# A hybrid encoder layer: one-hot picks per tile in the router's pipeline, and attention's levels ahead of the layer norm's tail

## What is computed

```
h = rms_norm(x);  q,k,v,r,gates,glu = split(h @ w_in)
a = gated linear attention, both directions, 4 heads, per-head norm, times silu(r)
b = silu(layer_norm(depthwise_conv31(glu_a * sigmoid(glu_g))))
x = x + concat(a, b) @ w_out
x = x + cross_attention(rms_norm(x), rms_norm(mem))      # 4 heads
h = rms_norm(x)
logits = h @ router_w + router_b                          # 1024 x 32
top_vals, top_idx = top_k(logits, 4);  gates = softmax(top_vals)
# tokens sorted by expert into blocks of rows; each block goes through its expert:
hid = min(g,7) * sigmoid(1.702 * min(g,7)) * (clip(l,-7,7) + 1)   # g,l = halves of x @ w_up[e] + b_up[e]
x = x + sum over the 4 picks of gate * (hid @ w_down[e] + b_down[e])
y = rms_norm(x)
```

## Time and profile before

| | us |
|---|---|
| median of 3 runs | 2631.83 (2628.87 to 2635.72) |
| profiled execution, own time | 2631.96 |
| its span in the trace | 2630.2 |
| TensorE busy | 2385.0 (91%) |
| VectorE busy | 1825.1 (69%) |
| ScalarE busy | 1286.7 (49%) |
| GpSimd busy | 363.0 (14%) |

### The profile page before, as it was taken

How to read it: one execution, slowest core, us unless ns; L and a number is a source line. 1 busy time by engine, 2 the same in 40 slices (tenths; PEclk the granted TensorE clock), 3 DMA queues, 4 the chain that set the end, 5 groups by cost and what they waited for, 6 DMA issues and landing times.

```text
span 2630.2 us, 38944 instructions
## 1 busy us (share of the span) xinstructions
PE 2385.0 (91%) x13604; PEld 1936.6 (74%) x13605; DVE 1825.1 (69%) x1912; ACT 1286.7 (49%) x1435; POOL 363.0 (14%) x305
## 2 busy tenths in 40 slices
PE   6999886699979967999999999999999999999993
PEld 4889664598748945777777777787787777777772
DVE  4699678514142276878977778778777788988763
ACT  5412255313231133656756565556565556766553
POOL 0000000010000032121212111121122112222111
PEclk7999998799999868999999999999999999999996
DMA  4211311310100138989988797789787789999775
GB/s 139 64 49 49 113 34 34 129 57 33 48 1 1 51 108 308 310 305 327 359 282 266 252 319 251 235 269 331 258 276 243 242 294 312 337 362 314 250 248 160
DMA packets 263969, 527.23 MB, mean 200 GB/s; under 512 B 10909, under 2 KB 45009, under 8 KB 263537
## 3 DMA queue, kind: packets, MB, share of 16 engines
q1 hardware_dynamic: 246976, 470.49, 50.9%
q0 software_dynamic: 15008, 52.70, 8.7%
q10 hardware_dynamic: 1904, 2.90, 0.4%
HBM read 484.37 MB, written 41.68 MB: 200 GB/s over the span
## 4 chain that ended last, share of the span: by engine, by line
PE 78%; DVE 10%; issue 5%; ACT 4%; DMA 1%; DVEq 1%; ACTq 0%; POOLq 0%; POOL 0%; SPq 0%
PE PS L2497 12%; PE PS L2499 11%; PE PS L2498 11%; PE PS L2064 9%; PE PS L2505 7%; PE PS L2502 6%; PE PS L2296 4%; PE PS L2394 4%; DVE wlo L1856 2%; PE PS L2467 1%; PE PS L2356 1%; PE PS L2321 1%; PE PS L2322 1%; PE PS L2323 1%; PE PS L2521 1%
## 5 line engine op out<-in xcount | busy, mean ns | idle before, releaser
L1856 DVE TENSOR_TENSOR wlo<-raw,whi 128x2048 fp32r<-128x2048 f32 x387 | 880.0, 2288 | 198.6 <-ACT whi L1116 175.7
L1116 ACT CAST whi<-raw 128x2048 fp32r<-128x2048 f32 x387 | 730.5, 1911 | 177.1 <-PE PS L2505 137.2
L2497 PE MATMUL PS<-whi,xhi 128*128 128x512 f32 x1024 | 426.2, 416 | 1.0 <-DVE wlo L1856 0.9
L2499 PE MATMUL PS<-whi,xlo 128*128 128x512 f32 x1024 | 401.6, 392 | 0.0
L2498 PE MATMUL PS<-wlo,xhi 128*128 128x512 f32 x1024 | 400.2, 391 | 0.3 <-issue 0.3
L2499 PEld LDWEIGHTS PS<-whi,xlo 128*128 128x128 f32 x1024 | 193.0, 188 | 42.5
L2497 PEld LDWEIGHTS PS<-whi,xhi 128*128 128x128 f32 x1024 | 194.4, 190 | 39.9 <-DVE wlo L1856 6.4
L2498 PEld LDWEIGHTS PS<-wlo,xhi 128*128 128x128 f32 x1024 | 193.6, 189 | 39.4 <-issue 0.8
L2497 PE MATMUL PS<-whi,hhi 128*128 128x512 f32 x512 | 203.2, 397 | 8.7 <-DVE wlo L1856 8.7
L2499 PE MATMUL PS<-whi,hlo 128*128 128x512 f32 x512 | 200.1, 391 | 0.0
L2498 PE MATMUL PS<-wlo,hhi 128*128 128x512 f32 x512 | 199.8, 390 | 0.0
(11 more groups left out here) (400 smaller groups left out, 4568.9 us busy)
## 6 DMA issues: line engine op xcount, KB each, us to landing
raw<-in_exp_w_up SPq DMA_DIRECT2D x259, 1024.0 KB
raw<-in_exp_w_down SPq DMA_DIRECT2D x128, 1024.0 KB
ring<-in_w_in SPq DMA_DIRECT2D x11, 1024.0 KB, 5.4
xres<-in_x SPq DMA_DIRECT2D x4, 1024.0 KB, 10.4
ring<-in_xattn_wk SPq DMA_DIRECT2D x4, 1024.0 KB, 9.1
ring<-in_xattn_wv SPq DMA_DIRECT2D x4, 1024.0 KB, 4.9
ring<-in_w_out SPq DMA_DIRECT2D x4, 1024.0 KB, 7.1
xres<-in_x SPq DMA_DIRECT2D x1, 4096.0 KB, 20.7
```

What stands on the lines that cost most here:

```text
L1116: nc.scalar.copy(whi[:, chunk_slot(c, NSPL), :], raw[chunk_slot(c, NRAW)][:]).then_inc(s_whi, 1)
L1856: nc.vector.tensor_tensor(wlo[:, chunk_slot(c, NSPL), :], raw[chunk_slot(c, NRAW)][:], whi[:, chunk_slot(c, NSPL), :].bitcast(F), ALU.subtract
L2497: pe.matmul(o, hi[:, k, :], wh, start=first and bias is None, stop=False)
L2499: ins = pe.matmul(o, lo[:, k, :], wh, start=False, stop=stop and kk == 3)
```

## The change

It has four parts.

1. Attention's levels and the layer norm: VectorE makes the first exponents and the product with the sigmoid of r ahead of the variance; the inverse comes in level 2, the scalings in levels 3 and 4, the gating after the queries' products. ScalarE takes the sigmoid of r first, the root in level 1, the gains in levels 4 and 5 and the sigmoids after level 6, and drains memory halves between the levels. TensorE starts the scores after the means and does a whole memory chunk behind each of the levels 1 to 5.
2. In the norms of cross attention and router, ScalarE copies the transposes of tile t - 4 ahead of squaring tile t.
3. The bias loads and the router's parameter loads are issued after the first product of the output projection, and GpSimd's parts start there; bias parts, router weights and biases get other places in SBUF (`rw` 188, `rbb` 143.875, `bdn` 193 KiB).
4. The one-hot picks are made per tile inside the router's loop. The steps of the tables are reordered: visit starts and visit table, then gates, then rows; on TensorE the visit product comes ahead of the bias transposes. The tables have four buffers each, and ScalarE multiplies by the token id.

The core of the diff; what it leaves out only moves instructions into the functions named here, or into the order just told.

Sizes and places:

```diff
-RT_M, RT_GD, RT_LO, RT_VD, RT_VT = 9, 17, 27, 36, 42
+RT_VD, RT_VT, RT_GD, RT_LO = 19, 23, 28, 34
+        NTAB = 4
-        rowhot = sb("rowhot", [P, 2, TOPK, P], F, 168)
-        blkhot = sb("blkhot", [P, 2, TOPK, 2, NB], F, 176)
+        rowhot = sb("rowhot", [P, NTAB, TOPK, P], F, 152)
+        blkhot = sb("blkhot", [P, NTAB, TOPK, 2, NB], F, 163)
-        bstage = sb("bstage", [P, 2 * FF], F, 152)
+        bstage = sb("bstage", [P, 2 * FF], F, 133)
```

GpSimd:

```diff
-            pool.wait_ge(s_mm["o"], 32)
+            pool.wait_ge(s_mm["o"], 1)
             nc.gpsimd.memset(onesb[:], 1.0).then_inc(s_rmi, 1)
```

ScalarE:

```diff
+            act.wait_ge(s_mm["in"], 70)
+            act.wait_ge(s_dr["in"], 70)
+            nc.scalar.activation(SR[:], r_tm[:], ACT.Sigmoid).then_inc(s_sr, 1)
             for c in range(CT):
                 act.wait_ge(s_lnv, 2 * (c + 1))
                 nc.scalar.activation(o_gla[:, 2 * c:2 * c + 2, :], yT[:, c, :].rearrange("p (a b) -> p a b", a=2),
                                      ACT.Square).then_inc(s_lna, 1)
...
-            drain_memory(range(4))
-            nc.scalar.activation(SR[:], r_tm[:], ACT.Sigmoid).then_inc(s_sr, 1)
-            drain_memory(range(4, 8))
             window_decays(0)
+            drain_memory((0, 1))
             for l in range(7):
                 exps(0, l)
+                if l == 1:
+                    conv_root()
                 if l == 2:
                     place_halves(0)
                 if l == 3:
                     place_quarters(0)
-                if l >= 3:
-                    drain_memory((5 + l,))
+                if l in (4, 5):
+                    conv_gain((2 * l - 8, 2 * l - 7))
+                drain_memory((2 * l + 2, 2 * l + 3) if l < 6 else (14,))
+            conv_sigmoid()
             exps(0, "ends")
-            drain_memory((12,))
+            drain_memory((15,))
             place_diagonal(0)
-            drain_memory((13,))
             exps_from_starts(0)
-            drain_memory((14, 15))
             keys_turned(0)
             window_decays(1)
             exps(1, "ends")
             exps_from_starts(1)
+            act.wait_ge(s_lnv, 19)
             drain_values(0, range(4))
...
             y_square(0)
             for t in range(1, TT):
+                if t >= 4:
+                    hidden_states_hi(t - 4)
                 y_square(t)
                 y_root(t - 1)
-                if t >= 4:
-                    hidden_states_hi(t - 4)
...
-            for c in range(1, 4):
-                split_wo(c)
-
-            act.wait_ge(s_mm["o"], 24)
+            split_wo(1)
+            act.wait_ge(s_mm["o"], 1)
+            for i in range(3):
+                act.dma_start(bstage[E * i:E * (i + 1), :], A["exp_b_up"][0]).then_inc(s_bld, 16)
+            for i in range(3):
+                act.dma_start(bdn[E * i:E * (i + 1), :], A["exp_b_down"][0]).then_inc(s_bld, 16)
             act.dma_start(gfb[:], A["norm_ffn_g"][0].partition_broadcast(P)).then_inc(s_rpar, 16)
             act.dma_start(rw[:], A["router_w"][0].rearrange("(k p) e -> p k e", p=P)).then_inc(s_rpar, 16)
             act.dma_start(rbb[:], A["router_b"][0].partition_broadcast(P)).then_inc(s_rpar, 16)
+            split_wo(2)
+            split_wo(3)
...
             z_square(0)
             for t in range(1, TT):
+                if t >= 4:
+                    h3_turned_out(t - 4)
                 z_square(t)
                 z_root(t - 1)
-                if t >= 4:
-                    h3_turned_out(t - 4)
             z_root(TT - 1)
-            act.wait_ge(s_mm["o"], 32)
-            for i in range(3):
-                act.dma_start(bdn[E * i:E * (i + 1), :], A["exp_b_down"][0]).then_inc(s_bld, 16)
-            for i in range(3):
-                act.dma_start(bstage[E * i:E * (i + 1), :], A["exp_b_up"][0]).then_inc(s_bld, 16)
             for t in range(TT - 4, TT):
                 h3_turned_out(t)
             act.wait_ge(s_bld, 6 * 16)
+            act.wait_ge(s_bup, 8)
             nc.scalar.copy(bdn3[:], bdn[:]).then_inc(s_gx, 1)
...
             for n in range(EARLY_BASE):
                 base_rows(n)
+            for t in range(TT):
+                act.wait_ge(s_oh, 2 * t + 1)
+                nc.scalar.mul(blkhot[:, t % NTAB, :, 0, :], blkhot[:, t % NTAB, :, 0, :], pid[:, t:t + 1]
+                              ).then_inc(s_ids, 1)
```

VectorE:

```diff
+            conv_variance()
             for l in range(7):
...
                 if l in DIAG:
                     select(0, l)
+                if l == 2:
+                    conv_inverse()
+                if l in (3, 4):
+                    conv_scale((2 * l - 6, 2 * l - 5))
             keys_to_ends(0)
             select(0, 7)
             queries_from_starts(0)
+            conv_gate()
...
-            for t in range(TT + 5):
+            def one_hot(t):
+                dve.wait_ge(s_top, 2 * t + 2)
+                nc.vector.tensor_copy(IXf[:, t, :], IX[:, t, :]).then_inc(s_hot, 1)
+                dve.wait_ge(s_hot, 4 * t + 1)
+                nc.vector.tensor_tensor(OH[:, t], iot[:, 0:E].unsqueeze(1).broadcast_to([P, TOPK, E]),
+                                        IXf[:, t, 0:TOPK].unsqueeze(2).broadcast_to([P, TOPK, E]), ALU.is_equal
+                                        ).then_inc(s_hot, 1)
+                dve.wait_ge(s_hot, 4 * t + 2)
+                two = slice(2 * (t % 4), 2 * (t % 4) + 2)
+                nc.vector.tensor_tensor(M[:, two, :], OH[:, t, 0:2, :], OH[:, t, 2:4, :], ALU.add).then_inc(s_hot, 1)
+                dve.wait_ge(s_hot, 4 * t + 3)
+                nc.vector.tensor_tensor(Mb[:, t, :], M[:, two.start, :], M[:, two.start + 1, :], ALU.add
+                                        ).then_inc(s_hot, 1)
+            for t in range(TT + 6):
...
-                if t >= 5:
+                if 5 <= t <= TT + 4:
                     logits(t - 5)
-            dve.wait_ge(s_top, 2 * TT)
+                if t >= 6:
+                    one_hot(t - 6)
+            dve.wait_ge(s_hot, 4 * TT)
...
-            step(nc.vector.tensor_copy(IXf[:], IX[:]))
-            for k in range(TOPK):
-                step(nc.vector.tensor_tensor(OH[:, :, k, :], iot[:, 0:E].unsqueeze(1).broadcast_to([P, TT, E]),
-                                             IXf[:, :, k:k + 1].broadcast_to([P, TT, E]), ALU.is_equal))
-            step(nc.vector.tensor_tensor(M[:], OH[:, :, 0, :], OH[:, :, 1, :], ALU.add))
-            step(nc.vector.tensor_tensor(M[:], M[:], OH[:, :, 2, :], ALU.add))
-            step(nc.vector.tensor_tensor(Mb[:], M[:], OH[:, :, 3, :], ALU.add))
...
-                nc.vector.tensor_scalar(ids, ids, pid[:, t:t + 1], None, ALU.mult).then_inc(s_oh, 1)
```

TensorE:

```diff
-            pe.wait_ge(s_lnv, 10)
...
+            pe.wait_ge(s_lnv, 8)
             scores(0, 0)
             memory_chunk(1)
-            memory_chunk(2)
-            memory_chunk(3)
-            for l in range(1, 8):
+            pe.wait_ge(s_lnv, 10)
+            for l in range(1, 6):
                 scores(0, l)
-                memory_chunk(4 + (l - 1) // 2, ((l - 1) % 2,))
-            memory_chunk(7, (1,))
+                memory_chunk(l + 1)
+            for l in (6, 7):
+                scores(0, l)
+                memory_chunk(7, (l - 6,))
...
-            pe.wait_ge(s_rt, RT_M)
+            pe.wait_ge(s_hot, 4 * TT)
...
             for t in range(TT):
                 pe.wait_ge(s_oh, 2 * t + 2)
+                pe.wait_ge(s_ids, t + 1)
```

More of the change, by code:

```diff
@@ L1794, in _ @@
             assert rt == RT_VD
+            dve.wait_ge(s_gx, 2)
+            step(nc.vector.tensor_reduce(gsum[:, 0, :], Gt[:], X, ALU.add))
+            step(nc.vector.reciprocal(gsum[:, 1, :], gsum[:, 0, :]))
+            step(nc.vector.tensor_tensor(Gt[:], Gt[:], gsum[:, 1, :].unsqueeze(2).broadcast_to([P, TT, TOPK]),
+                                         ALU.mult))
+            dve.wait_ge(s_rk, 3)
+            step(nc.vector.tensor_copy(VT[:].rearrange("p a v -> p (a v)"), PS[:, 5, 0:2 * NV]))
+            assert rt == RT_VT
+            tA = tmpA[:]
+            for k in range(TOPK):
+                step(nc.vector.tensor_tensor(tA[:, :, k, :], OH[:, :, k, :],
+                                             Gt[:, :, k:k + 1].broadcast_to([P, TT, E]), ALU.mult))
+            step(nc.vector.tensor_reduce(GD[:], tA.rearrange("p t k e -> p t e k"), X, ALU.add))
+            assert rt == RT_GD
             step(nc.vector.tensor_tensor(slot0[:], PS[:, 6, 0:TT * E].rearrange("p (t e) -> p t e", e=E),
```

120 lines of the change are left out of this document (56 added, 64 removed).

## The result

The changed kernel takes 2601.71 us in the median of 4 runs (2599.99 to 2605.41), the kernel before 2633.77 (4 runs, 2628.87 to 2640.43) beside it: a ratio of 0.988, 95% interval 0.9862 to 0.9898, 32 us less. The forecast was 2592.8, with 2583 to 2613 as its range. The profiled execution of after took 2605.41 us (span 2603.6); against the profiled one of before (2631.96, span 2630.2) that is only 26.6 us less. The two differences, 32 and 26.6, are both to be explained.

The account below looks back on a forecast made before the run. TensorE, busy 91% of the span, was taken as the bound, with gains only where it idles or runs at 1.2 GHz. 10.5 + 0.3 + 15.4 + 16.7 - 3.7 = 39.2 us off 2631.96 gave 2592.8, range 2583 to 2613.

Parts of the forecast that it names:

- The levels (10.5): Attention's levels ahead of the layer norm's tail: waits vanish and state updates start earlier, gain 10.5 us.
- the walk: Instruction-by-instruction timing of the new engine orders; in attention from 311.4 us, it put the states at 389.0.
- Rival 1: Attention part yields nothing, as drains and two more table loads keep VectorE waiting; 2603 us, chance 0.14.
- rival 3: Attention's levels: TensorE falls to 1.2 GHz and the kernel gets slower; 2656 us, chance 0.04.
- The norms (15.7): Copies ahead of squares: 0.3 us in cross attention's norm, 15.4 in the router's by shorter TensorE rounds.
- Rival 2: Low clock stays in the router, losing 14 us in the rounds and 8 in the tail; 2614.8, chance 0.20.
- Tail and picks (16.7): From the last projection tile to the end of the one-hot picks: 37.7 us becomes 21.0, gain 16.7.
- Tables (-3.7): Making the tables after the picks: TensorE's table products start later and end at 40.7 us, loss 3.7.
- The experts (0): Expert visits start 39 us earlier and keep their length, so nothing is gained or lost there.
- Rival 4: Expert stage's loads, not the visit table, set its pace and eat the gain; 2632 us, chance 0.04.

Follow-up runs that it names:

- fill: The changed kernel plus three unused f32 products in TensorE's idle time ahead of head pair 1's values; 2601.06 us, ratio 0.9872.
- before_fill: The kernel before plus three unused f32 products in TensorE's idle time ahead of head pair 1's values; 2633.33 us, ratio 0.9992.
- picks_last: The changed kernel with all eight one-hot groups issued behind the last tile's maximum; 2599.60 us, ratio 0.9865.
- picks_gaps2: The changed kernel with only tile 0's one-hot group left in the rounds, the others behind later router maxima; 2596.01 us, ratio 0.9848.
- picks_gaps: The changed kernel with the one-hot groups of tiles 0 and 1 left in the rounds, the other six behind router maxima; 2600.43 us, ratio 0.9869.
- no_levels: The changed kernel with its first part undone, so the layer norm's tail is again ahead of attention's levels; 2615.17 us, ratio 0.9918.
- after_again: The changed kernel run once more without any edit; 2599.86 us.
- copies_only: The kernel before with only the copies of turned tokens put ahead of the squares in both norms; 2623.69 us, ratio 0.9954.

## Why the prediction held, and where it was off

**The levels (10.5): right.** A is 10.3 to 10.4 us shorter in all pairs. VectorE followed the walk within 1 us: level 4 was forecast for 350.5 and came at 350.66; the states for 389.0, and came at 389.84, in an execution that is 0.8 us late at the layer norm already. The 1.0 us set aside for a low clock at the state updates was not needed there: VectorE's 28 updates take 10.33 us, before 10.32. A like sum was lost further on. Counted from the layer norm the states are 11.5 us early, the values of head pair 1 only 10.3; that the two figures meet is luck. Rival 1 is out, and rival 3, since TensorE's chunks keep full speed (clock 0.92). Table loads cost what the row said: the sigmoids end, a load takes 1.28, the exponential starts.

```profile
368.69 4.63 ACT L842 ACTIVATE yT<-yT,PV 128x1024 f32<-128x1024 f32 x4
373.34 1.28 ACT L867 ACT_TABLE_LOAD   x1
374.63 2.00 ACT L867 ACTIVATE EX<-EX 128x1024 f32<-128x1024 f32 x2
```

The drain of about 1.38 us that the Trainium skill (ScalarE: Activation LUTs, What ACT_TABLE_LOAD costs) adds shows in none of the five loads; the measurement decides.

**What the levels gain was not carried to the end.** I stopped at the states and took it for granted that 10.5 us arrives at the sum. Behind them B took 6.6 of it back in the profiled pair. That is not the change's doing. The profile of before happened to be one with an early rise (12.9), that of after one with none (19.5). The same code without fillers gave 19.1 and 19.5 in other profiles with the old levels, and 13.4, 15.0, 17.5, 19.1 and twice 19.5 with the new ones; the means are 17.1 and 17.6. That it is also why the profiled pair differs by 26.6 us and the medians by 32 is likely, but not shown: the other executions of the two have no profile, and fill, whose B is short, has no lower median.

**The norms (15.7): 18.05 in the profiled pair, of which 15.6 are the rounds.** The rounds are 15.6 shorter (35.1 to 19.5, by the windows), forecast 15.4. The swap in the cross attention's norm was put at 0.3. The other 2.5 lie between the first w_out product and these rounds, and 1.7 of them in front of the second tile of the q products: in before a q product of 512 columns came every 0.43 us there until 616.5, in after every 0.23 us from the second on (610.25, 610.49, 610.72). That looks like the swap's doing and is not. before_fill has no swap and full speed at this place, picks_last has the swap and a low clock (609.33 to 609.75):

```profile
612.46 0.39 PE L2327 MATMUL PS<-hL,wqH 128*128 128x512 f32 x1
612.69 0.40 PE L2328 MATMUL PS<-hH,ringL 128*128 128x512 f32 x1
```

```profile
609.33 0.63 PE L2352 MATMUL PS<-hL,wqH 128*128 128x512 f32 x1
609.75 0.57 PE L2353 MATMUL PS<-hH,ringL 128*128 128x512 f32 x1
```

So the clock here is a chance of the execution as in B. Outside the rounds D takes 373.1 to 375.1 us in three profiles without the swap and 371.4 to 374.0 in eleven with it. Between the means of all profiles D is 17 us shorter, 1 more than forecast. Rival 2 did not happen in the rounds.

**Tail and picks (16.7): 13.4.** Two things were mis-sized. I had set aside 4.0 us for a clock that is low in part; it was low for all router products but the first. The walk itself was good at both ends: at full clock it gave 17.0 us (923.0 less 906.0), and picks_gaps2 has 16.8; with a low clock it gave 25.0 (931 less 906.0), and after has 24.3. And I put the pipelined group at one late microsecond on the last mean, which is what it costs, but not what follows: root, copy, a wait of TensorE, the clock. Rival 2's mechanism came true here, released by the change itself. Without GpSimd beside it a group is 0.9 us and its comparison 0.29, about as forecast. The bias parts now run beside the projection, and the additions there, which read PSUM, stay at 0.42 us.

```profile
814.60 8.26 POOL L596 TENSOR_TENSOR bstage<-bstage,bup 32x2048 f32<-32x2048 f32 x2
```

```profile
816.71 0.42 DVE L1615 TENSOR_TENSOR xres<-xres,PS 128x256 f32<-128x256 f32 x1 [2.46 <-PE PS L2424]
```

The Trainium skill (SBUF — State Buffer, Who interferes with whom) says that a VectorE instruction with at most one input in SBUF, outside its two-port modes, does not contend with GpSimd. These rows agree: 0.42 us in the middle of GpSimd's 8.26.

**Tables (-3.7): -4.1.** TensorE's first table product came 28.9 us behind the last pick (27.5 forecast), the last one ended at 41.3 (40.7).

**The experts (0): -3.5.** The step "the expert visits start 39 us earlier and keep their length" failed. The tokens come 30.1 us earlier, the end 26.6. H is 1620.7 to 1624.8 with the old tables (four profiles), and 1624.2 to 1627.6 with the ids on ScalarE (seven); with them back on VectorE it is 1619.4 to 1623.2 (three). So the cost comes with the ids on ScalarE, which the sum had put at nothing behind the tables: the prediction saw the later weight casts and let the wait for the gathered tokens cover them. Rival 4 had the place right and the size wrong; its mechanism, the loads, is not shown. Within the second set H spreads by 3 us. TensorE got 180 to 183 instructions done in the first 60 us at clock 0.83 in after, picks_gaps and picks_gaps2 (1624.2 to 1624.5), 166 to 169 at 0.77 to 0.80 in fill, picks_last and no_levels (1626.8 to 1627.6), and 175 at 0.77 in after_again (1625.0). The share of the DMA engines is 0.83 to 0.86 in the first three and 0.80 or 0.81 in the others. Whether the clock or the loads lead here is open.

**The sum.** The means of all profiles with the same code in a stretch make an estimate without the chance of one pair: A 10.4, B -0.5, D 16.9, E 13.4, F -4.2, G -0.3, H -3.2, together 32.5 us. The medians gave 32, and 37 when after was repeated beside another set of before. So of the forecast 39.2 us some 3.3 failed in the tail's clock and 3.2 in the experts. Only D ran the other way, by 1 us: the result is inside the range because the range was wide enough.

**Left open.** copies_only measured 10.9 us; its stretches, with an equal B on both sides, would give 15 to 16. Whether its executions all fell on a late rise isn't known, since one of them has a profile. What decides when the clock rises in B isn't shown. That fill's 6 us in B don't reach its median was seen, and only 3 of it found (in H).

## What to carry to other kernels

Follow a gain to the next place where TensorE restarts after waits, and look there at the clock; compare two profiles of the same kernel before you explain a difference of a few us: here one stretch varied by 6 us in the same program. A small operation put "into the pipeline" costs by what is queued behind it on its engine: list who waits for the next instruction, two engines further on, and place it behind the last producer instead, and look again. Where several microseconds hang on the clock, a few unused products in an idle stretch ahead are a cheap test of it.

## What was unexpected of the hardware

The same instructions in the same program ran at 1.2 GHz for 18.5 us without a wait in one execution (after, granted 0.50) and at 2.4 GHz from 4.6 us on in another (after_again). With three f32 products of 128x512 in the idle stretches ahead, four profiles of four show 2.4 GHz from the first product, and the length of the stretch is then 11.26 to 11.33 us. In the router's tail, with its products of 32 columns, a wait of 0.36 us left the clock at 1.00 in all three kernels that had it (a product takes 1.97 us); a wait of 1.25 us at the same place was followed by 0.50 in all seven profiles that had it (3.62 us). The length of the wait alone is not the rule: in before, whose clock had been low in the rounds and came back to 1.00 just ahead of the tail, waits of 1.87 and 1.31 us at this place left both products at full speed.

```profile
928.27 1.97 PE L2380 MATMUL PS<-rw,h3T 128*128 128x32 f32 x16 [1.31 <-ACT h3T L1074]
```
